# Rotating queries and keys in transposed form instead of by rows

## What is computed

```
q, k = x @ w[:, QA:QA+1024], x @ w[:, KA:KA+1024]      (256 tokens, 16 heads of 64)
r1, r2, rest = t[..., 0:8], t[..., 8:16], t[..., 16:64]
t = concat(r1 * cos - r2 * sin, r1 * sin + r2 * cos, rest)
scores = q k^T / 8, softmax by chunks
```

## Time and profile before

| | us |
|---|---|
| median of three runs (2759.63 to 2759.92) | 2759.65 |
| the profiled execution | 2758.44 |
| its span, first to last instruction | 2756.6 |
| TensorE busy in it | 2742.8 |
| VectorE busy | 1821.8 |
| ScalarE busy | 1464.0 |
| GpSimd busy | 213.0 |

### The profile page before, as it was taken

How to read it: one execution, slowest core, us unless ns; L and a number is a source line. 1 busy time by engine, 2 the same in 40 slices (tenths; PEclk the granted TensorE clock), 3 DMA queues, 4 the chain that set the end, 5 groups by cost and what they waited for, 6 DMA issues and landing times.

```text
span 2756.6 us, 44844 instructions
## 1 busy us (share of the span) xinstructions
PE 2742.8 (99%) x18188; PEld 2453.3 (89%) x18188; DVE 1821.8 (66%) x2892; ACT 1464.0 (53%) x2404; POOL 213.0 (8%) x156
## 2 busy tenths in 40 slices
PE   9999999999999999999999999999999999999998
PEld 8989879989989779989988887899899898878997
DVE  6656765646656866656577878775565678787755
ACT  5445655445455645445456566454444565665542
POOL 0010001010010011010012100110100121001100
PEclk9999999999999999999999999999999999999999
DMA  6544445555544445555545344555555554445553
GB/s 247 198 170 163 151 161 189 194 184 199 199 169 152 149 174 200 199 196 199 199 182 195 142 181 148 212 201 194 192 199 194 197 184 153 162 167 184 213 199 123
DMA packets 75069, 504.10 MB, mean 183 GB/s; under 512 B 8784, under 2 KB 10480, under 8 KB 19184
## 3 DMA queue, kind: packets, MB, share of 16 engines
q1 hardware_dynamic: 74576, 501.06, 50.7%
q10 hardware_dynamic: 288, 0.17, 0.0%
HBM read 500.12 MB, written 1.08 MB: 182 GB/s over the span
## 4 chain that ended last, share of the span: by engine, by line
PE 98%; DVE 1%; DMA 0%; issue 0%; ACT 0%; SPq 0%; DVEq 0%
PE ps L1668 48%; PE ps L1688 43%; PE ps L1709 3%; PE ps L1804 1%; PE ps L1802 1%; PE ps L1829 1%; DVE wlo L2167 1%; PE ps L1831 0%; PE ps L1853 0%; DVE g L2378 0%; DMA raw<-in_w 0%; PE ps L1703 0%; PE ps L1820 0%; PE ps L1821 0%; PE ps L1819 0%
## 5 line engine op out<-in xcount | busy, mean ns | idle before, releaser
L1904 ACT ACTIVATE whi<-raw 128x1024 fp32r<-128x1024 f32 (+3 forms) x938 | 976.5, 1043 | 611.5 <-PE ps L1668 400.4
L2167 DVE TENSOR_TENSOR wlo<-raw,whi 128x1024 fp32r<-128x1024 f32 (+2 forms) x894 | 1080.8, 1216 | 273.7 <-ACT whi L1904 272.6
L1688 PE MATMUL ps<-xT_both,whi 128*128 128x256 f32 x6848 | 856.8, 278 | 0.0
L1688 PEld LDWEIGHTS ps<-xT_both,whi 128*128 128x128 f32 x6848 | 813.0, 188 | 6.8 <-issue 5.3
L1668 PE MATMUL ps<-whi,xT_both 128*128 128x512 f32 (+2 forms) x2176 | 586.7, 390 | 2.2 <-ACT whi L1904 1.8
L1668 PEld LDWEIGHTS ps<-whi,xT_both 128*128 128x128 f32 x2176 | 396.2, 188 | 79.8 <-issue 6.6
L1688 PE MATMUL ps<-xT_both,wlo 128*128 128x256 f32 x3424 | 459.3, 277 | 0.0
L1688 PEld LDWEIGHTS ps<-xT_both,wlo 128*128 128x128 f32 x3424 | 421.2, 188 | 0.0
L1668 PE MATMUL ps<-wlo,xT_both 128*128 128x512 f32 (+2 forms) x1088 | 331.2, 385 | 0.3 <-DVE wlo L2167 0.3
L1668 PEld LDWEIGHTS ps<-wlo,xT_both 128*128 128x128 f32 x1088 | 202.1, 188 | 39.1 <-DVE wlo L2167 1.4
L1668 PE MATMUL ps<-whi,hT_hi 128*128 128x512 f32 x704 | 221.4, 390 | 0.0
(11 more groups left out here) (306 smaller groups left out, 2119.8 us busy)
## 6 DMA issues: line engine op xcount, KB each, us to landing
raw<-in_w SPq DMA_DIRECT2D x435, 1024.0 KB, 4.8
vr<-in_vrows SPq DMA_DIRECT2D x19, 512.0 KB, 5.6
raw<-in_w SPq DMA_DIRECT2D x12, 768.0 KB, 4.3
raw<-in_w SPq DMA_DIRECT2D x10, 896.0 KB, 4.5
sums<-scratch SPq DMA_DIRECT2D x8, 512.0 KB, 4.4
raw<-in_w SPq DMA_DIRECT2D x4, 832.0 KB, 4.4
raw<-in_w SPq DMA_DIRECT2D x4, 576.0 KB, 3.7
raw<-in_w SPq DMA_DIRECT2D x4, 512.0 KB, 7.2
```

Of the source, the lines that this page charges most:

```text
L1688: made = e.matmul(out, ws[:, o:o + 128], xs[:, kt, :], start=kt == 0 and n == 0 and c % 2 == 0, stop=kt == job.nk - 1 and n == 2, skip_gro ...
L1904: e.activation(out, raw, ACT.Copy).then_inc(*mark("hi", i))
L2167: e.tensor_tensor(out, raw, hi.bitcast(F32), sub).then_inc(*mark("lo", i))
```

## The change

The rotated chunks are made by columns, so that no transposes are needed. For each pair of heads (a bank of 128x512: two groups of 128 dimensions by 256 tokens) ScalarE writes the bank into `rot` with neighbouring groups of 32 partitions exchanged, in four copies of 32x512. VectorE multiplies the bank by a cosine table straight into `qka`, multiplies the exchanged copy by a sine table in place, and adds the two. For this each head's columns of the weights are put into another order on the host (dimensions 0 to 7, 16 to 39, 8 to 15, 40 to 63), so that the two halves of the rotated part lie 32 partitions apart; queries and keys have the same order, so their products are the same. The table grows from 2x32 to 2x256 numbers per partition, the buffers `rot_t` go, and the scratch that the program reserves for dynamic DMAs shrinks from 8192 to 4096 bytes per partition.

```
 def place(key):
-    if key[0] in ("qk1", "z", "xbc", "qc", "kc"):
+    if key[0] in ("qk1", "z", "xbc", "qa", "ka", "qc", "kc"):
         return COLUMNS_AT
...
-    sbuf("rope2", [128, 2, 32])
+    sbuf("rope2", [128, 2, 256])
...
-            many("rot_t", 2, [128, 128], F32, reg2)
...
-            toks = self.gemm((name, l, n), xt, 8, [[(b, 0, 512)] for b in banks], free)
+            outs = [banks[i // 2][:, 256 * (i % 2):256 * (i % 2) + 256] for i in range(4)]
+            tok = self.gemm_w((name, l, n), xt, 8, outs, free)

             def post():
-                bufs = []
-                for t in (0, 1):
+                for j in (0, 1):
                     buf, b_free = rot.get()
-                    self.do("rope2", name, l, n, t, banks[t], toks[t], buf, b_free)
-                    self.main.put(banks[t], ("vec", "rope2", name, l, n, t))
-                    bufs.append(buf)
-                yield
-                yield
-                for k in (0, 2):
-                    ps, p_free = self.aux.get()
-                    self.do("rope2_turn", name, l, n, k, base + 4 * n + k, bufs, ps, p_free, qka)
-                    self.aux.put(ps, ("copy_a", "qka", l, base + 4 * n + k))
-                    if k == 0:
-                        yield
-                for t in (0, 1):
-                    rot.put(bufs[t], ("tr", "rope2", name, l, n, 2))
+                    hh = base + 4 * n + 2 * j
+                    self.do("rope2", l, hh, banks[j], tok, buf, b_free, qka[:, hh:hh + 2, :])
+                    self.main.put(banks[j], ("vec", "cosine", l, hh))
+                    rot.put(buf, ("vec", "rot", l, hh))
+                    yield
...
 scalar_program
-    def rope2(name, l, n, t, bank, tok, buf, free):
+    def rope2(l, hh, bank, tok, buf, free, _):
         act.wait_ge(*at(*tok))
         for f in free:
             act.wait_ge(*at(*f))
-        e.activation(buf[:, :], bank[:, :], ACT.Copy).then_inc(*mark("copy_a", "rope2", name, l, n, t))
-
-    def rope2_turn(name, l, n, k, hh, bufs, ps, free, qka):
-        act.wait_ge(*at("tr", "rope2", name, l, n, k))
-        e.activation(qka[:, hh:hh + 2, :].rearrange("p a b -> p (a b)"), ps[:, :], ACT.Copy
-                     ).then_inc(*mark("copy_a", "qka", l, hh))
+        for g in range(4):
+            made = e.activation(buf[32 * g:32 * g + 32, :], bank[32 * (g ^ 1):32 * (g ^ 1) + 32, :], ACT.Copy)
+        made.then_inc(*mark("copy_a", "swapped", l, hh))
...
 vector_program
+    def rope2(l, hh, bank, tok, buf, free, out):
+        dve.wait_ge(*at("copy_a", "swapped", l, hh))
         dve.wait_ge(*at("rope2"))
...
+        e.tensor_tensor(out, bank[:, :].rearrange("p (a b) -> p a b", a=2), bc1(m["rope2"][:, 0, :], 2), mul
+                        ).then_inc(*mark("vec", "cosine", l, hh))
+        b3 = buf[:, :].rearrange("p (a b) -> p a b", a=2)
+        e.tensor_tensor(b3, b3, bc1(m["rope2"][:, 1, :], 2), mul).then_inc(*mark("vec", "sine", l, hh))
+        dve.wait_ge(*at("vec", "sine", l, hh))
+        e.tensor_tensor(out, out, b3, add).then_inc(*mark("vec", "rot", l, hh))
```

More of the change, by code:

```diff
@@ L1358, in heads_a @@
                              for j in (0, 1)],
-                            (("copy_a", "qka", l, h - h % 2), ("copy_a", "qka", l, 8 + h - h % 2)))
+                            (("vec", "rot", l, h - h % 2), ("vec", "rot", l, 8 + h - h % 2)))
                     probs[s] = self.scores(("a2", l, s), banks[s], 0.125, m["chunk"][:, :], ("chunk",),
@@ L1607, in tables2 @@
         e.dma_start(m["chunk"][:, :], bias_d[6]).then_inc(*mark("chunk", by=16))
-        e.dma_start(m["rope2"][:, :, :], rope_d[:, :, 64:96]).then_inc(*mark("rope2", by=16))
+        e.dma_start(m["rope2"][:, :, :], rope_d[:, :, 64:320]).then_inc(*mark("rope2", by=16))
     def vrow(i, n, row, freed):
@@ L1765, in mla_turn @@
         made.then_inc(*mark("tr", "mlaT", l, h))
-    def rope2_turn(name, l, n, k, at_, bufs, ps, free, _):
-        for f in free:
-            pe.wait_ge(*at(*f))
-        for t in (0, 1):
-            pe.wait_ge(*at("vec", "rot", name, l, n, t))
-        for j in (0, 1):
-            for t in (0, 1):
-                made = transpose(ps[:, 256 * j + 128 * t:256 * j + 128 * t + 128],
-                                 bufs[t][:, 128 * (k + j):128 * (k + j) + 128])
-        made.then_inc(*mark("tr", "rope2", name, l, n, k))
     def conv_out(l, ct, acc, ps, free):
@@ L2505, in halve_b @@
         made.then_inc(*mark("xlo", *key))
-    rotated = []
-    def rope2(name, l, n, t, bank, tok, buf, free):
-        p3 = bank[:, :].rearrange("p (h d) -> p h d", h=8)[:, :, 0:16]
-        d3 = buf[:, :].rearrange("p (h d) -> p h d", h=8)
-        a3, b3 = (r[:, :].rearrange("p (h d) -> p h d", h=8) for r in m["rot_t"])
-        dve.wait_ge(*at("copy_a", "rope2", name, l, n, t))
-        dve.wait_ge(*at("rope2"))
-        if rotated:
-            dve.wait_ge(*at(*rotated.pop()))
-        e.tensor_tensor(a3, p3, bc1(m["rope2"][:, t, 0:16], 8), mul)
-        e.tensor_tensor(b3, p3, bc1(m["rope2"][:, t, 16:32], 8), mul).then_inc(*mark("vec", "rope2", name, l, n, t))
-        dve.wait_ge(*at("vec", "rope2", name, l, n, t))
-        e.tensor_tensor(d3[:, :, 0:8], a3[:, :, 0:8], b3[:, :, 8:16], sub)
-        e.tensor_tensor(d3[:, :, 8:16], a3[:, :, 8:16], b3[:, :, 0:8], add).then_inc(*mark("vec", "rot", name, l, n, t))
-        rotated.append(("vec", "rot", name, l, n, t))
+    def rope2(l, hh, bank, tok, buf, free, out):
+        dve.wait_ge(*at("copy_a", "swapped", l, hh))
+        dve.wait_ge(*at("rope2"))
+        e.tensor_tensor(out, bank[:, :].rearrange("p (a b) -> p a b", a=2), bc1(m["rope2"][:, 0, :], 2), mul
[4 more added lines that the diff above has]
+        e.tensor_tensor(out, out, b3, add).then_inc(*mark("vec", "rot", l, hh))
     def diff(l, h, p0, p1, d0, d1, r, nlam):
@@ L2698, in constants, with rotary_order @@
     c1, s1, c2, s2 = np.cos(a1), np.sin(a1), np.cos(a2), np.sin(a2)
-    rope = np.concatenate([c1, c1, s1, s1, c2, c2, s2, s2], axis=1).astype(f)
-    rope = np.ascontiguousarray(rope.reshape(2, 128, 96).transpose(1, 0, 2))
-    return np.eye(128, dtype=f), bias, msk, rope
+    rope = np.zeros((128, 2, 320), f)
+    rope[:, :, 0:64] = np.concatenate([c1, c1, s1, s1], axis=1).reshape(2, 128, 64).transpose(1, 0, 2)
+    rope[:, 0, 64:] = 1.0
+    for first in (0, 64):
+        rope[first:first + 8, 0, 64:] = rope[first + 32:first + 40, 0, 64:] = c2.T
+        rope[first:first + 8, 1, 64:] = -s2.T
+        rope[first + 32:first + 40, 1, 64:] = s2.T
+    return np.eye(128, dtype=f), bias, msk, rope
+def rotary_order():
+    order = np.arange(GP + 3072)
+    head = np.r_[0:8, 16:40, 8:16, 40:64]
+    for first in range(QA, QA + 1024, 64):
+        order[first:first + 64] = first + head
+    for first in range(KA, KA + 1024, 64):
+        order[first:first + 64] = first + head
+    return order
 def kernel(**inputs):
@@ L2710 @@
     a = {k: _np.ascontiguousarray(v) for k, v in inputs.items()}
+    a["w_mix_in_2"] = _np.ascontiguousarray(a["w_mix_in_2"][:, :, rotary_order()])
     blocks = place_pieces()
```

6 lines of the change are left out of this document (3 added, 3 removed).

## The result

Median of 6 runs: 2775.05 us (2772.94 to 2778.75), against 2759.64 before (6 runs). The ratio is 1.0055, with a 95% interval of 1.0045 to 1.0066: the change makes the kernel slower by 15.4 us. The forecast was 2771.3, 11.6 slower; the result lies inside its range.

The account below looks back on a forecast made before the run. TensorE bounds the kernel, but late decay tables from VectorE, ScalarE and GpSimd would make it wait: 6.7 less 0.87 is 5.8 us a layer, +11.6 for two, on 2759.65: 2771.3 us, range 2766 to 2776 (0.70).

Parts of the forecast that it names:

- The mechanism: Rotation work on ScalarE and VectorE is in series with the decay tables, so tables come late and TensorE waits.
- Rounds: Times between GpSimd's table products grow by 2.84, 2.16 and 2.16 us, making the fourth table 7.2 us later.
- the bound of 0.59 each: ScalarE's exchange copies: 0.48 us start to start expected, 2.03 per half chunk; upper bound 0.59 each, without overlap.
- The waits: TensorE waits 1.3 us at the second scan product, 3.9 at the third, about as long before the fourth.
- VectorE's half: Rotating half a chunk on VectorE takes three 128x512 operations, 1.95 us, in place of four short ones.
- The fourth scan product: On TensorE it moves from 1533.00 to 1539.7, 6.7 us later; less 0.87 for transposes behind it, 5.8 net per layer.
- rival 3: TensorE's clock falls in the waits: fourth product about 2 us later per layer, 2775.5 us, or 2780; chance 0.08.
- my signs of being wrong: No TensorE wait at the scan product or normalising product, exchange copies well under 0.5 us, or a falling granted clock.
- TensorE's gain: Dropping 64 transposes in 16 groups saves 3.4 us per layer, 6.9 for both; column pieces cost nothing extra.
- Rival 4: VectorE, 1 to 4 us behind at the attention heads, holds TensorE 0 to 1.5 us a layer; within the forecast's 0.70.
- Row against rule: VectorE operations with two SBUF inputs contend with GpSimd's table product; new sine product and sum just miss it, sum unchanged.
- the ring: Queue orders on ScalarE and VectorE make exchange, rotation, table sum and minimum, and next exponential wait for each other.

Follow-up runs that it names:

- the filled wait: Changed kernel with 12 TensorE products of 128x512 put ahead of the third scan product's wait for its table: 2775.37 us, ratio 1.0059.
- the run with the square alone: Changed kernel with only ScalarE's square of the scan output moved, behind the exchange of the next chunk's first half: 2769.71 us, ratio 1.0027.
- the run with the product on VectorE: Changed kernel with the square behind the exchange and the decay table product moved from GpSimd to VectorE, ahead of the scan output: 2758.04 us, ratio 0.9995.
- four orders that keep the product on GpSimd: Changed kernel, 2775.05 us; it with the square one step later, 2775.18; with scan output sooner and square behind the exchange, 2770.1; with only that square move, 2769.71.

## Why the prediction was right, and where its steps were off

**The mechanism was right.** The rotation lies in series with the decay tables, the rounds grow, TensorE starts to wait at the table and at the normalising product, and the transposes saved are lost in the wait. Taking two of VectorE's three operations away brings the stage back under its old length (-0.72), and taking the whole rotation away brings it to -2.86 with no wait; so the cause is shown and not only argued.

**Rounds.** Forecast longer by 2.84, 2.16, 2.16; measured 3.15, 2.52, 2.52 (the old ones being 14.29, 14.31 and 15.36). Together 8.19 and not 7.16. The mis-sized term is ScalarE's exchange. Its copies take 0.59, as forecast, but a group of four takes 2.40 and not 2.03: one starts 0.60 behind the other, with no overlap, so the bound of 0.59 each was the true value. That is 0.37 in each round, against a difference of 0.31, 0.36 and 0.36: it explains the whole of it. ScalarE in the second round of the changed kernel:

```profile
1508.58 2.39 ACT L2092 ACTIVATE rot<-ps 32x512 f32<-32x512 f32 x4
1511.00 1.06 ACT L1884 ACTIVATE whi<-raw 128x1024 fp32r<-128x1024 f32 x1
```

The two copies of 128x512 before overlapped (1.07 for two). The Trainium skill, page "ScalarE: Activation LUTs", section "What ACT_TABLE_LOAD costs", says that activations in a row overlap by about 93 ns; these copies do not, and the measurement decides. Why copies between partition groups of 32 differ was not tried.

**The waits** were forecast at 1.3 at the second product, 3.9 at the third and about as much before the fourth. In the first layer they are 1.22, 3.65 and 1.13 + 0.44. The last is smaller because slow operations of TensorE fill the rest: from the third scan product's start to the end of the column group behind it (1527.99 to 1534.73) it took 6.74 us, 2.36 more than behind the first (1497.08 to 1501.46). So the waits are 6.4 us in the first layer and 6.9 in the second, and not 9.

**VectorE's half** was forecast at 1.95 and is 1.94 (cosine at 1494.17, low half at 1496.11).

**The fourth scan product** was forecast 6.7 later. In the first layer it is at 1545.96, less the 5.25 by which the whole stage is late, 1540.71: 7.7 later. Less 0.87 behind it gives +6.8, and the stage measures +6.86. The step from table to stage holds; the excess is the exchange's.

**The second layer** has 1.05 more, and that is rival 3, the clock. There the clock falls behind the normalising product too (first window of 4 us at 0.86, second at 0.71), and this time nothing covers it. TensorE in the second layer:

```profile
2313.95 0.71 PE L1856 MATMUL ps<-ident,stat 128*128 128x128 f32 x4 [2.00 <-POOL stat L2575]
2314.41 1.66 PE L1659 MATMUL ps<-whi,xT_both 128*128 128x512 f32 x4
...
2316.72 1.81 PE L1659 MATMUL ps<-whi,xT_both 128*128 128x512 f32 x4
...
2318.93 0.65 PE L1833 MATMUL ps<-decay,xd 128*64 128x256 f32 x4
```

The table was ready at 2314.31 + 3.47 = 2317.78, and the product comes 1.15 later, without a wait. From the normalising product it took 4.98 us where the first layer took 3.92, 0.44 of waiting included. I had given the clock 2 us a layer or nothing; it fell in both layers, and cost 1.05 in one. A falling clock was one of my signs of being wrong, and on this point the forecast was: it put the clock at nothing. The error of the rival was to add the price of the low clock to the late chain: where another wait follows, the two share their time, as the filled wait shows; where none follows it costs 1.0 to 1.5 a layer (the filled wait, the run with the square alone).

**TensorE's gain** was forecast at 3.4 a layer, with 0 for slow column pieces and a bound of 0.1 each. It is 2.86. Behind the first scan product column pieces take 2.83 (1501.46 to 1504.29) and keep that until the next interruption; behind the second they do so in the changed kernel, but are back at 2.72 after one piece in the kernel without the rotation (1508.07, 1510.91, 1513.63). The missing 0.57 a layer is put down to such pieces by this count, not by a run of its own. The value 0 was the wrong end.

**Sum.** By the forecast's terms: exchange +1.0, slower pieces covered by waits, low clock +1.05 in one layer: 5.8 becomes 6.8 and 7.9, as measured. Rival 4, lateness behind the fourth product, is not seen: no wait at the heads.

**Row against rule.** I had said that the sine product and the sum would just miss GpSimd's product. In the changed kernel they do (676 to 683 ns), and the forecast lost nothing by it. That was partly luck: by the forecast's own times the sine product would start at s + 5.00, 0.06 before the table product is over. With the exchange longer than forecast it starts at s + 5.48 (1511.62), 0.44 behind it. But I read this as the rule having no part in the sum. The runs show that it has one as soon as anything in the ring is shortened. VectorE's own work in a round is 12.4 us (two halves of 1.93, four low halves of 1.14, 1.73, 0.67 and 1.58); some 9.8 of that has two SBUF inputs, and GpSimd's product is 3.5. If the two exclude each other throughout, no order can bring a round under 13.3 (an estimate from these durations), while TensorE came round in 12.54 in the run with the product on VectorE. In four orders that keep the product on GpSimd the second round was 16.83, 17.38, 15.69 and 15.25; these lie well above the bound, and what keeps them there is which operation is held, and what waits for it. In the changed kernel the product hit nothing only because VectorE stood idle for 4.4 us then, waiting for the exchange.

## What to carry over

When a chain runs through two engines that exclude each other, add their times before looking for a better order: an order mostly chooses which operation is held, and moving the work to the engine that is already busier can shorten the round (14.57 in place of 15.25 us). Look also at the small operations in the same queues: one short root, held and late, was worth more than the rounds (a wait of 3.02 us became 0.55). Price work that is taken off the bound engine by what its suppliers get in exchange, and read their margins (here 3.3 us down to 0.5) before its busy share. A wait that disappears in one place is gained only if the next late thing has slack: follow every moved step to the end of the stage and a little beyond.

## What was not expected of the hardware

- ScalarE's copies of 32x512 between partition groups take 589 ns each and 2.40 us in fours, without overlap; two of 128x512 take 1.07.
- VectorE and GpSimd hold each other up by whole instructions: 3.29 us for an operation of 0.42, 5.66 for two of 1.22, 4.48 for GpSimd's 3.51, and 1.61 for a root of 0.70.
- A run of column pieces has two forms, 2.72 and 2.83 us each. The slow one can last some 100 us; in some executions it adds about 4 us to the same code, in the old kernel with the smaller scratch and in the new one alike. What selects it stays open.
- Behind a wait of 3.65 us the granted clock was 0.50 for a stretch of 4 us; behind one of 1.22 us it did not fall (1.00 from 1511 to 1515), nor behind one of 1.13, and behind one of 2.00 it did (0.71). The same wait of some 3.03 us was followed by a fall in one layer and by none in the other, in two kernels.
